# A decoder layer on one core: result strips turned by VectorE block transposes and SBUF-to-SBUF transfers instead of TensorE transposes

## What is computed

```python
h = rmsnorm(x, g_mix[i]);  proj = h @ w_in[i]           # q, k, v, indexer, gates
out_a = dsa_sparse_attention(...)                        # 8 heads, 64 keys picked by an indexer
out_b = forgetting_attention(...)                        # 8 heads
mixed = sigmoid(gate_a) * (out_a @ w_o_a[i]) + sigmoid(gate_b) * (out_b @ w_o_b[i])
x = x + mixed @ w_out[i]
h = rmsnorm(x, g_ffn[i])
x = x + (silu(h @ w_ffn_gate[i]) * (h @ w_ffn_up[i])) @ w_ffn_down[i]     # inner width 5632
h = rmsnorm(x, g_ple[i])
x = x + sigmoid(h @ w_ple_gate[i]) * (p[i] @ w_ple_proj[i])
return rmsnorm(x, g_final)
```

## Time and profile before

| | |
|---|---|
| median of 3 runs | 1509.48 us (1509.47 to 1509.54) |
| span of the profiled execution | 1507.6 us; the time around it is not listed apart, the median is 1.88 us above the span |
| mean granted TensorE clock | 0.998 of full speed |
| PE busy | 1479.9 us, 98% |
| PEld, DVE, ACT | 1241.4, 856.2, 692.2 us |
| DMA | 278.87 MB, mean 185 GB/s |

### The profile page before, as it was taken

One profiled execution on the slowest core, in us unless ns is written; L12 is line 12 of the kernel. 1 busy time (PEld: TensorE's weight loads), 2 busy tenths in 40 slices (PEclk: granted clock), 3 DMA queues, 4 the chain that ended last, 5 costly groups with the idle time before them and its releaser, 6 DMA issues.

```text
span 1507.6 us, 19536 instructions
## 1 busy us (share of the span) xinstructions
PE 1479.9 (98%) x7025; PEld 1241.4 (82%) x7025; DVE 856.2 (57%) x988; ACT 692.2 (46%) x846; POOL 50.0 (3%) x80
## 2 busy tenths in 40 slices
PE   5999999999999999999999999999999999999996
PEld 5888888888888888888888888888888888888885
DVE  6966776657655566555445454444545454454554
ACT  5644444544444544545444444444444343443544
POOL 0021001100210000000000000000000000000000
PEclk9999999999999999999999999999999999999999
DMA  6666565566555665566666666566666666666663
GB/s 191 183 195 176 170 197 177 164 186 195 173 168 168 184 197 184 182 191 187 191 185 193 185 194 192 184 191 185 193 184 193 190 187 195 187 190 195 196 211 111
DMA packets 164910, 278.87 MB, mean 185 GB/s; under 512 B 12856, under 2 KB 50160, under 8 KB 164336
## 3 DMA queue, kind: packets, MB, share of 16 engines
q1 hardware_dynamic: 164112, 274.98, 59.8%
q10 hardware_dynamic: 736, 3.03, 0.5%
HBM read 275.87 MB, written 2.11 MB: 184 GB/s over the span
## 4 chain that ended last, share of the span: by engine, by line
PE 96%; DVE 2%; DMA 1%; ACT 0%; issue 0%; DVEq 0%; ACTq 0%
PE acc L1206 51%; PE acc L1211 25%; PE acc L1102 8%; PE acc L1111 4%; PE side L1206 2%; PE side L1211 1%; PE side L1307 1%; DMA rope_c<-in_rope_rows 1%; DVE ls L676 1%; PE side L1252 0%; DVE hn L731 0%; PE side L1258 0%; PE side L1266 0%; PE side L1267 0%; PE side L1265 0%; PE acc L1307 0%
## 5 line engine op out<-in xcount | busy, mean ns | idle before, releaser
L676 DVE TENSOR_TENSOR ls<-ws,hs 128x1024 fp32r<-128x1024 f32 (+1 forms) x520 | 634.0, 1226 | 584.9 <-ACT hs L384 581.6
L384 ACT ACTIVATE hs<-ws 128x1024 fp32r<-128x1024 f32 (+1 forms) x520 | 548.0, 1057 | 737.8 <-PE acc L1211 610.6
L1206 PE MATMUL acc<-hs,xg 128*128 128x512 f32 x1648 | 408.3, 390 | 0.0
L1206 PEld LDWEIGHTS acc<-hs,xg 128*128 128x128 f32 x1648 | 308.5, 188 | 63.4
L1211 PE MATMUL acc<-ls,xg 128*128 128x512 f32 x824 | 220.3, 389 | 0.0
L1211 PEld LDWEIGHTS acc<-ls,xg 128*128 128x128 f32 x824 | 154.7, 188 | 32.2
L1206 PE MATMUL acc<-hs,ff 128*128 128x512 f32 x704 | 174.3, 390 | 0.0
L1206 PE MATMUL acc<-hs,hn 128*128 128x512 f32 (+1 forms) x704 | 171.8, 387 | 0.0
L1206 PEld LDWEIGHTS acc<-hs,ff 128*128 128x128 f32 x704 | 131.9, 188 | 27.2
L1206 PEld LDWEIGHTS acc<-hs,hn 128*128 128x128 f32 x704 | 127.1, 188 | 24.2
L1102 PE MATMUL acc<-hn,hs 128*128 128x512 f32 x560 | 139.2, 392 | 0.0
(11 more groups left out here) (195 smaller groups left out, 825.5 us busy)
## 6 DMA issues: line engine op xcount, KB each, us to landing
ws<-in_w_in SPq DMA_DIRECT2D x152, 512.0 KB, 4.0
ws<-in_w_ffn_gate SPq DMA_DIRECT2D x88, 512.0 KB, 3.5
ws<-in_w_ffn_up SPq DMA_DIRECT2D x88, 512.0 KB, 3.5
ws<-in_w_ffn_down SPq DMA_DIRECT2D x88, 512.0 KB, 3.6
ws<-in_w_out SPq DMA_DIRECT2D x32, 512.0 KB, 3.7
ws<-in_w_ple_gate SPq DMA_DIRECT2D x32, 512.0 KB, 4.2
ws<-in_w_o_b SPq DMA_DIRECT2D x16, 512.0 KB, 4.2
ws<-in_w_o_a SPq DMA_DIRECT2D x16, 512.0 KB, 4.1
```

Source lines behind the costliest of these rows:

```text
L384: act.activation(hs[:, j, 0:n], ws[:, j, 0:n], ACT.Copy).then_inc(h_split, 1)
L676: dve.tensor_tensor(ls[:, j, 0:n], ws[:, j, 0:n], hs[:, j, 0:n].bitcast(F32), ALU.subtract).then_inc(l_split, 1)
L1206: pe.matmul(banks[b], src[:, k, part * TOK + b * P:part * TOK + (b + 1) * P], hs[:, slot, q * width:(q + 1) * width], start=first and q == ...
```

## The change

The transposes of `columns_of` go. Instead VectorE turns each result strip in blocks of 32 x 32 within its partition groups (`turn_quads`: two instructions into `t_rows`, one per token block, written with a step of two numbers so that the two blocks interleave). Then 16 transfers of 32 partitions x 256 numbers (32 KB each) put each block into the partition group where it belongs, from `t_rows` to `t_cols` (`move_quads`): eight issued by SP and eight by ScalarE. ScalarE and VectorE then take the high and low part from `t_cols` in SBUF instead of from PSUM. The order of the tokens within a tile is now interleaved: token n of block b lies at 2n + b. TensorE picks a block of `mixed`, `xg` and `ff` by a step of two numbers (`block_of`), while `hn`, `heads_o` and `p_cols` stay contiguous. `t_cols` shares its place with `mix_b` and `ff_tok`, so VectorE waits for the low part of the strip before ahead of writing these. `sq` and `p_tok` move to other addresses. Three loops of SP are written out, and the FFN loop of TensorE has five rounds rather than four and two strips ahead of it.

```diff
+QUAD = 32
+QUADS = P // QUAD
+MOVES = QUADS * QUADS
...
+    t_cols = sb("t_cols", 184, [QUADS, 4, QUAD, 2])
+    t_rows = sb("t_rows", 196, [QUADS, 4, QUAD, 2])
...
+        return t[:, :, :, :, :].rearrange("p a k n b -> p k a (n b)")
...
+    def move_quads(eng, t, odd):
+
+        eng.wait_ge(turned, 2 * t + 2)
+        for a in range(QUADS):
+            for q in range(odd, QUADS, 2):
+                eng.dma_start(t_cols[QUAD * q:QUAD * (q + 1), a, :, :, :],
+                              t_rows[QUAD * a:QUAD * (a + 1), q, :, :, :]).then_inc(moved, 16)
...
                     load(c % SLOTS, w[:, KW * c:KW * (c + 1), ds(i * WIDE, WIDE)])
+                if half == 0:
+                    move_quads(sp, T_FF - 1 + i, 0)
...
+        def split_and_move(first, t):
+
+            split_chunks(first, 2)
+            move_quads(act, t, 1)
+            split_chunks(first + 2, 2)
...
-            act.wait_ge(xg_t, 4 * stage + n + 1)
+            act.wait_ge(moved, 16 * MOVES * ((T_X, T_PLE)[stage] + n + 1))
...
-            for j in range(SLOTS):
-                split_high(u + 1, j)
+            split_high(u + 1, 0)
+            split_high(u + 1, 1)
+            move_quads(act, T_FF - 1 + c, 1)
+            split_high(u + 1, 2)
+            split_high(u + 1, 3)
...
+        def turn_quads(rows, at):
+
+            for b in range(2):
+                dve.transpose(t_rows[:, :, :, :, b].rearrange("p q k n -> p k q n"),
+                              rows[:, b, at:at + WIDE].rearrange("p (k q n) -> p k q n", k=4, q=QUADS)).then_inc(turned, 1)
...
             dve.tensor_tensor(x_tok[:, :, cols], acc[:, 2 * pair:2 * pair + 2, :], x_tok[:, :, cols], ALU.add).then_inc(x_new, 1)
+            dve.wait_ge(x_new, 4 * stage + n + 1)
+            turn_quads(x_tok, WIDE * n)
...
+        def block_of(src, k, part, b):
+
+            if src is hn or src is heads_o or src is p_cols:
+                return src[:, k, part * TOK + b * P:part * TOK + (b + 1) * P]
+            return src[:, k, part * TOK:(part + 1) * TOK].rearrange("p (n b) -> p b n", b=2)[:, b, :]
...
-        def columns_of(rows, bank, at, ready):
-
-            for m in range(4):
-                for b in range(2):
-                    mm = pe.transpose(bank[m // 2][:, m % 2 * TOK + b * P:m % 2 * TOK + (b + 1) * P],
-                                      rows[:, b, at + m * P:at + (m + 1) * P], ident[:, :])
-            mm.then_inc(ready, 1)
```

More of the change, by code:

```diff
@@ L289, in _ @@
         wide_columns(U_GB, N_WIDE, win_t, AT_GB)
-        with sp.Fori(0, N_WIDE) as i:
+        for i in range(N_WIDE):
             for c in range(K_CH):
@@ L293, in _ @@
                 w, t = (wob_t, woa_t)[c // SLOTS], KW * (c % SLOTS)
-                load(c % SLOTS, w[:, t:t + KW, ds(i * WIDE, WIDE)])
+                load(c % SLOTS, w[:, t:t + KW, WIDE * i:WIDE * (i + 1)])
+            if i > 0:
+                move_quads(sp, T_MIX + i - 1, 0)
         sp.wait_ge(o_ready, FREE + HEADS)
         sp.dma_start(p_tok[:, :, :], p_rows).then_inc(p_loaded, 16)
-        wide_columns(U_OUT, N_WIDE, wout_t, 0)
+        for i in range(N_WIDE):
+            for c in range(K_CH):
+                slot_free(U_OUT + c // SLOTS + i * 2, c % SLOTS)
+                load(c % SLOTS, wout_t[:, KW * c:KW * (c + 1), WIDE * i:WIDE * (i + 1)])
+            move_quads(sp, T_MIX + N_WIDE - 1 + i, 0)
         with sp.Fori(0, N_FFN) as i:
@@ L537, in _ @@
             cols = slice(WIDE * n, WIDE * (n + 1))
-            split_chunks(C_WO + 8 * n + 4, 4)
-            if n > 0:
+            if n == 0:
+                split_chunks(C_WO + 4, 4)
+            else:
+                split_and_move(C_WO + 8 * n + 4, T_MIX + n - 1)
                 mixed_high(n - 1)
@@ L961, in _, with new_low @@
             dve.tensor_tensor(mix_b[:, :, :], mix_b[:, :, :], mix_a[:, :, :], ALU.add).then_inc(mix_s, 1)
-        def new_low(stage, n, pair):
+            dve.wait_ge(mix_s, n + 1)
+            turn_quads(mix_b, 0)
+        def new_low(stage, n):
             for m in range(4):
@@ L1009, in ff_pair @@
             else:
-                ff_low(c - 1, (step + 1) % 2)
+                ff_low(c - 1)
             for j in range(SLOTS):
@@ L1018, in ff_pair @@
             dve.wait_ge(chunk_used, 4 * (u + 4))
+            if first:
+                dve.wait_ge(xg_ready, KT)
+            else:
+                dve.wait_ge(ff_ready, c)
             for b in range(2):
@@ L1205, in high_part @@
                     for part in range(2):
-                        pe.matmul(banks[b], src[:, k, part * TOK + b * P:part * TOK + (b + 1) * P],
+                        pe.matmul(banks[b], block_of(src, k, part, b),
                                   hs[:, slot, q * width:(q + 1) * width], start=first and q == 0 and part == 0, stop=False)
@@ L1233, in closing_chunks @@
                         w_h, w_l = (t[:, slot, q * WIDE:(q + 1) * WIDE] for t in (hs, ls))
-                        x_h, x_l = (src[:, k, part * TOK + b * P:part * TOK + (b + 1) * P] for part in range(2))
+                        x_h, x_l = (block_of(src, k, part, b) for part in range(2))
                         pe.matmul(banks[b], x_h, w_h, start=False, stop=False)
@@ L1326, in _ @@
                          c % SLOTS == 0, c % SLOTS == SLOTS - 1)
-                if c == HOOK and n > 0:
-                    mixed_columns(n - 1)
-        def new_columns(stage, n, pair):
-            pe.wait_ge(x_new, 4 * stage + n + 1)
-            columns_of(x_tok, pair_of(side, pair), WIDE * n, xg_t)
         for n in range(N_WIDE):
             if n < 2:
-                pe.wait_ge(mix_ready, n + 3)
+                pe.wait_ge(merged, 2 * n + 5)
             else:
@@ L1377, in ff_pair @@
                     by_token(at + K_CH * half + c, c % SLOTS, range(KW * c, KW * (c + 1)), xg, pair_of(acc, 1 - half), c == 0, c == K_CH - 1)
-                    if c == HOOK and half == 0:
-                        if first:
-                            new_columns(0, 3, 1)
-                        else:
-                            if reused:
-                                pe.wait_ge(ff_ready, pair_n - 2)
-                            ff_columns(pair_n - 1, (step + 1) % 2)
         ff_pair(0, 0, first=True)
-        ff_pair(0, 1, reused=False)
-        ff_pair(0, 2, reused=False)
-        with pe.Fori(1, (N_FFN - 1) // 2) as i:
+        with pe.Fori(0, (N_FFN - 1) // 2) as i:
             ff_pair(i, 1)
```

122 lines of the change are left out of this document (57 added, 65 removed).

## The result

The changed kernel takes 1515.76 us (median of 5 runs, 1515.71 to 1515.92), the kernel before 1509.48 us on the same chip (5 runs, 1509.46 to 1509.54). The ratio is 1.0042, interval [1.0031, 1.0053]. So it is 6.3 us slower, where 1489.1 us was forecast. Of the four runs of the contiguous version, further down, one took 3834.85 us; it is left out there and was not explained. The span is 1513.9 us, at a mean granted clock of 0.998 as before.

The account below looks back on a forecast made before the run. TensorE, busy 98% of the span, was taken as the bound. Removed transposes -20.7 us, loads, turn and issues 0, tight strips +0.3 gave -20.4 us: from 1509.5 to 1489.1 us, range 1486.5 to 1504.

Parts of the forecast that it names:

- The busy times, the waits, the lead: Whole kernel: TensorE, 98% busy, is the slowest link; ScalarE can be some 7 us late, VectorE more.
- What is removed: TensorE: eight transposes gone from each of 23 strips, 0.90 us a strip, 20.7 us saved, none of it waited for.
- tight strips: Last `mix_b` and last `x_tok` ahead of the FFN: transfers just fit before TensorE needs their columns; 0.3 us for both.
- The same matmuls with stepped stationary operands: 3936 TensorE matmuls of `mixed`, `xg`, `ff`: stepped loads stay hidden, cost 0, bounded from 0 to 425 us.
- that rival: Stepped loads of `mixed`, `xg`, `ff` become TensorE's bound: gain cancelled at 5.3 ns extra pitch, up to about 1914 us; chance 0.10.
- The turn on VectorE: Two VectorE instructions a strip, 0.74 us each, 34 us in all; VectorE about 890 us busy; hidden, cost 0.
- The issues: Eight DMA issues each on ScalarE and SP, 0.37 us each, 3.0 us for eight; covered by slack, cost 0.
- The transfers: 16 SBUF-to-SBUF transfers a strip, landing 3.6 us after issue, 65 us of engine time over 23 strips; overlapped and hidden.
- the second rival: Transfers run one after another, eight a queue at 3.6 us: 12.5 us in each of 23 strips, about 1776 us; chance 0.04.
- Sum: -20.7 + 0 (loads) + 0 (turn) + 0 (issues) + 0.3 = -20.4 us, giving 1489.1 us.

Follow-up runs that it names:

- contiguous version: The changed kernel with its turns and transfers, but the two token blocks kept apart so that every stationary operand is contiguous: 1489.86 us, ratio 0.9869 to the kernel before.
- table of four corners: Transposes on TensorE: contiguous operands 1509.45 us, step of two 1535.0. Turned by VectorE and transfers: contiguous 1489.86, step of two 1515.76.
- first probe: The kernel before with steps and widths of stationary operands varied by strip; only matmul start distances read: 226.7 ns at 512 columns, step 1; 233.3 at step 2.

## Why the prediction was wrong

**The busy times, the waits, the lead.** Right. TensorE was the bound and stayed it.

**What is removed: -20.7 us.** Right, nearly. The contiguous version gives -19.6. Its tight strips cost 1.5 us by the distance of chunk starts, which would leave -19.2; 0.4 us of gain is not accounted for. Outside those strips its chunk is 2.72 us.

**"The same matmuls with stepped stationary operands": 0.** This is the step that failed. It measures 6.7 ns x 3936 = 26 us (25.5 and 25.9 us in the table of four corners). It was bounded from 0 to 425 us, and I took 0 "because the row that it is nearest to has half of the budget free". That the load needs only about 110 ns was even true: with a step it needs 118. What was wrong is the inference that a load which has time enough costs the matmul nothing. Why it costs something is not shown; what the cost depends on is. Loads run beside the matmuls (83% and 98% of the span), and the runs show that the pitch of a 512-column matmul depends on where the stationary one lies, at 4 to 7 ns, long before the load is the limit.

The same text worked out that 5.3 ns of extra pitch cancel the gain: 2.3% of a matmul. With a break-even that near to the lower end, on 3936 instructions of the engine that bounds everything, "hidden" needed a row to 1%, and no row had a stepped load. The place and the break-even of that rival were right, its chance of 0.10 was too low, and its condition, over 222 ns from load to matmul, wasn't what decided: the load still starts one matmul ahead of its own and needs 118 ns. In the one case seen beyond that line, step 4, where a load needs 233 ns, the pitch at 512 columns is 235.

The Trainium skill ("SBUF — State Buffer", "Door 1: The DMA port swizzle") gives 16-byte lines, free at two hits each. For the load's own stream this case nearly agrees: at 128 columns a step of two costs 6 ns of 112, while a step of four, one hit a line, doubles the pitch (112 to 233 ns, and 120 to 233 at 256 columns). For 512-column matmuls it doesn't hold: a step of two costs 6.7 ns, and a contiguous load from a base 4, 16 or 32 numbers off, which hits every line four times, costs 5 to 6 ns. The measurement decides.

**The turn on VectorE: 0.** Right: 694 ns against 739 taken, in the changed kernel:

```profile
L989 DVE STREAM_TRANSPOSE t_rows<-ff_tok 128x512 f32<-128x512 f32 x22 | 14.4, 694 | 0.4
```

VectorE's 879.3 us are near the 890 forecast.

**The issues: 0.** The cost is right, the size was not: 0.59 and 0.61 us at the median instead of 0.37, near the 0.56 of the small loads; eight take 5.0 to 5.4 us (5.40 on ScalarE's queue in the last `mix_b` strip), not 3.0. I also placed the start of the FFN strip one chunk late. The transposes at 720.43 stand behind the fourth chunk, which started at 717.70, so that S was 717.70 - 3 x 2.72 = 709.54, and not 712.26; VectorE's product ended at S + 3.9. In the changed kernel S = 707.07, the issues of SP run from S + 5.3 to S + 10.6 instead of S + 2.8 to S + 6, and `hs` of chunk 6 starts at S + 11.0 instead of S + 9.8. The load of chunk 8 goes at S + 10.8, and ScalarE waits 0.91 us for it. Its slack of some 7 us covers all that, TensorE waits for none of it.

**The transfers: 0.** Right, and too careful: they land 1.9 us after issue, not 3.6, so the longer issues are made up for. The high part is taken at S + 12.9 (720.01), against S + 12 in the forecast and S + 19.7 as the latest. They don't run one after another: 16 of 1.9 us each would be 30 us, and all have landed 7.7 us after the first issue (712.34 to 720.01). So the second rival did not happen. (Its own sum was a little high too: S + 34 less S + 21.8 is 12.2 us, 281 us in 23 strips, not 288.) The Trainium skill's fixed cost of about 2 us ("SBUF — State Buffer", "The DMA setup-cost knee") agrees with the 1.9 us of one transfer, but 16 of them don't add up. The queue of SP went from 59.8% to 61.0% of the engines, and ScalarE's holds 2.0%:

```profile
q1 hardware_dynamic: 172944, 281.02, 61.0%
q10 hardware_dynamic: 9568, 9.07, 2.0%
```

**Two tight strips: +0.3.** Mechanism right, size a little off: TensorE waits 0.5 us for the last `mixed` in the changed kernel and 0.9 us in two places in the contiguous version; by the distance of chunk starts the strips cost 0.9 and 1.5 us. The low part of `mixed` was done at S + 17.9 (589.20, S = 571.30), not S + 16.5; TensorE had come to its chunk 6 at S + 17.45, after six chunks of 2.80. The issues took 2.4 us longer than forecast, which the sooner landing made up for in part.

**Sum.** All terms but one: -20.4 us forecast, -19.6 measured, 1489.1 against 1489.9 us. The one term: 0 against +26.

## What to carry to other kernels

On an engine that is 98% busy, an edit that touches the operands of every instruction is priced in per cents of one instruction times their count, before any gain elsewhere is counted; "it overlaps" is no price. Where a layout is free to choose, let the other engines do the odd strides and keep the stationary operand contiguous from a multiple of 64 float32 numbers: here that turned a loss of 6 us into a gain of 19.6. And when the gain cancels at 2% of a quantity that no row shows, the chance of the rival is not small.

## What the runs showed of the hardware that was not expected

- A 512-column float32r matmul whose stationary operand is contiguous from a multiple of 64 numbers starts every 226.7 ns. From bases 1, 2, 4, 8, 16, 32 or 96 numbers off it takes 231 to 233, at step 2 233.3, at steps 3, 4 and 8 235.5, 235 and 245. Counted in aligned pieces of 64 numbers that a load touches, these are 2, 3, 4, 6, 8 and 16. That this count is the cause is an inference from the series; steps 3 and 4 stand in the wrong order for it, and at step 4 the load's own 233 ns already explain most of the pitch. Why 256 to 448 columns pay at most 1 ns at step 2, and 496 columns 2 to 6 ns, stays open.
- The pitch of matmuls with loads at step 4 did not follow the granted clock. The 128-column ones ran from 1401.06 to 1649.06 us of the first probe. Between 1402 and 1403 us the granted clock fell from 1.00 to 0.50, the lower of its two levels (1.2 GHz), and it was at 1.00 again by 1653, in the 512-column strip behind them. The six matmuls that started ahead of the fall (1401.06 to 1402.22) are 234 ns apart, those at 0.50 233 ns, and the 256-column ones at step 4, at 1.00, 233 ns as well. Ahead of the strip TensorE had worked without a gap on 128-column matmuls at steps 1 and 2, at 1.00. The stretches of the first probe (128 columns at steps 1, 2, 4 and 4, then 256 columns at step 4; busy us by engine, granted clock, DMA share, GB/s):

```profile
1160.00:1170.00 10.00, 10.00 (x92) 10.00 (x91) 2.76 (x4) 2.12 (x2) 0.00 (x0) 1.00 0.33 109
1275.00:1395.00 120.00, 120.00 (x1022) 120.00 (x1022) 28.52 (x26) 24.91 (x29) 0.00 (x0) 1.00 0.29 95
1400.00:1510.00 110.00, 110.00 (x480) 110.00 (x479) 15.05 (x15) 13.25 (x18) 0.00 (x0) 0.51 0.15 51
1530.00:1640.00 110.00, 110.00 (x474) 110.00 (x473) 11.77 (x10) 10.57 (x10) 0.00 (x0) 0.50 0.15 48
1785.00:1805.00 20.00, 20.00 (x87) 20.00 (x87) 4.83 (x4) 5.46 (x8) 0.00 (x0) 1.00 0.27 91
```

- An issue of a 32 KB SBUF-to-SBUF transfer takes 0.51 us at least and 0.6 at the median on both SP's and ScalarE's queue, where the issue of a 512 KB load takes 0.37 us. The small transfer lands in 1.9 us.
